# Splitting the weights anew in every block instead of keeping the split ones in HBM

## What is computed

```python
proj = rmsnorm(x, norm1_g) @ w_in                 # x_a | x_b | g_a | g_b, 1024 columns each
c_a = causal_conv4(x_a);  y_a = rg_lru(c_a)       # gates from 8 heads of 128x128, a scan in time
y_b = grouped_matmul(window_means(x_b) - x_b, pool_w) * scale   # windows 2, 4, 8, 16
x = x + (sigmoid(g_a) * (y_a @ w_br_a) + sigmoid(g_b) * (y_b @ w_br_b)) @ w_out
gu = rmsnorm(x, norm2_g) @ w_gu                   # 2 x 2816 columns
x = x + (silu(gu[:, :2816]) * gu[:, 2816:]) @ w_down
y = rmsnorm(x, final_g)
```

## Time and profile before

| | |
|---|---|
| median of 3 runs | 3032.33 us (3031.15 to 3035.28) |
| the profiled execution | 3035.47 us, span of its instructions 3033.7 us |
| PE busy | 2927.4 us, 96% of the span |
| PE weight loads | 2855.7 us, 94% |
| DVE busy | 1377.6 us, 45% |
| ACT busy | 797.9 us, 26% |
| POOL busy | 306.1 us, 10%, all in the first quarter |
| moved by DMA | 746.61 MB, mean 246 GB/s |

### The profile page before, as it was taken

One profiled execution on the slowest core, in us unless ns is written; L12 is line 12 of the kernel. 1 busy time (PEld: TensorE's weight loads), 2 busy tenths in 40 slices (PEclk: granted clock), 3 DMA queues, 4 the chain that ended last, 5 costly groups with the idle time before them and its releaser, 6 DMA issues.

```text
span 3033.7 us, 36581 instructions
## 1 busy us (share of the span) xinstructions
PE 2927.4 (96%) x15150; PEld 2855.7 (94%) x15150; DVE 1377.6 (45%) x2312; ACT 797.9 (26%) x1281; POOL 306.1 (10%) x134
## 2 busy tenths in 40 slices
PE   6789999899999999999999999999999999999998
PEld 6788998888999999999999999999999999999998
DVE  7426555556433334463434435533344363333334
ACT  4634323323511111152221102611111034111001
POOL 4344444440000000000000000000000000000000
PEclk9899999999999999999999999999999999999999
DMA  7688898897666666666666666766666676566664
GB/s 279 210 286 315 306 322 298 285 309 282 231 230 249 234 223 233 226 250 229 234 246 232 225 232 226 253 228 238 242 231 227 229 252 235 215 231 234 230 230 176
DMA packets 124579, 746.61 MB, mean 246 GB/s; under 512 B 14080, under 2 KB 24576, under 8 KB 46336
## 3 DMA queue, kind: packets, MB, share of 16 engines
q1 hardware_dynamic: 114048, 728.82, 66.7%
q10 hardware_dynamic: 10368, 15.46, 1.4%
HBM read 603.37 MB, written 140.86 MB: 245 GB/s over the span
## 4 chain that ended last, share of the span: by engine, by line
PE 78%; DMA 10%; POOL 4%; DVE 3%; ACT 3%; issue 1%; SPq 1%; DVEq 0%; ACTq 0%
PE ps L292 77%; DMA wraw<-dwm 10%; POOL wring L252 4%; ACT wring L401 2%; SPq L222 0%; DVE tmp L731 0%; PE ps L310 0%; DVE tot L632 0%; DVE tmp L646 0%; DVE xlo L650 0%; DVE tmp L700 0%; DMA wring<-wsplit 0%; DVE rstd L637 0%; ACT L455 0%; ACT L473 0%
## 5 line engine op out<-in xcount | busy, mean ns | idle before, releaser
L292 PE MATMUL ps<-yhi,wring 128*128 128x420 f32 (+1 forms) x4800 | 1324.9, 354 | 19.1 <-DVE main L763 6.9
L292 PEld LDWEIGHTS ps<-yhi,wring 128*128 128x128 f32 x4800 | 904.0, 188 | 41.7 <-issue 13.4
L292 PE MATMUL ps<-xhi,wring 128*128 128x420 f32 (+1 forms) x3200 | 891.9, 356 | 35.0 <-POOL wring L252 20.7
L292 PE MATMUL ps<-ylo,wring 128*128 128x420 f32 (+1 forms) x2400 | 848.3, 353 | 0.0
L292 PEld LDWEIGHTS ps<-xhi,wring 128*128 128x128 f32 x3200 | 606.6, 190 | 54.2 <-POOL wring L252 24.4
L292 PE MATMUL ps<-xlo,wring 128*128 128x420 f32 (+1 forms) x1600 | 568.2, 355 | 0.0
L292 PE MATMUL ps<-hhi,wring 128*128 128x420 f32 (+1 forms) x1760 | 491.5, 355 | 15.7 <-POOL wring L252 14.3
L292 PEld LDWEIGHTS ps<-ylo,wring 128*128 128x128 f32 x2400 | 451.9, 188 | 8.6 <-issue 1.3
L292 PEld LDWEIGHTS ps<-hhi,wring 128*128 128x128 f32 x1760 | 332.4, 189 | 25.2 <-POOL wring L252 18.9
L252 POOL TENSOR_TENSOR wring<-wraw,wring 128x1024 fp32r<-128x1024 f32 x122 | 294.9, 2420 | 382.6 <-ACT wring L401 382.6
L763 DVE TENSOR_TENSOR main<-ps,main 128x420 f32<-128x420 f32 (+1 forms) x440 | 250.8, 590 | 136.7 <-PE ps L292 135.8
(11 more groups left out here) (94 smaller groups left out, 1681.7 us busy)
## 6 DMA issues: line engine op xcount, KB each, us to landing
wring<-wsplit SPq DMA_DIRECT2D x488, 1024.0 KB, 4.8
wsplit<-wring SPq DMA_DIRECT2D x122, 1024.0 KB, 5.0
wraw<-dwm SPq DMA_DIRECT2D x122, 512.0 KB, 5.9
sring<-ssplit SPq DMA_DIRECT2D x32, 512.0 KB, 3.9
dy<-main ACTq DMA_DIRECT2D x32, 210.0 KB, 6.1
xres<-dx ACTq DMA_DIRECT2D x28, 210.0 KB, 4.7
ssplit<-sring SPq DMA_DIRECT2D x8, 512.0 KB, 6.8
sraw<-dws SPq DMA_DIRECT2D x8, 256.0 KB, 7.1
```

Of the source, the lines that this page charges most:

```text
L292: mm = nc.tensor.matmul(out, wt[:, c * P:(c + 1) * P], x, start=(first and q == 0), stop=(last and q == 2))
```

## The change

The HBM scratch is gone, with its stores and loads. Every block loads raw slots, now into three buffers, and splits them itself: the high part on ACT, the low part on POOL. The sides likewise. `ahead` works in every block. In the heads stage and the feed-forward part some of its calls move: the split for the slot four after `ga(2p)` comes before ACT's wait for the scans, the one for `gb(p-1)` before the square roots, the one for the first `g` before `root`. The normalization for the next block is done in two halves, in rounds 5 and 6 of the feed-forward part instead of all in round 5. The SP queue issues raw loads in order, each after POOL is done with the slot three before.

```diff
+RAW = 3
...
-        wraw = sb("wraw", [P, 2, KT * P])
+        wraw = sb("wraw", [P, RAW, KT * P])
...
             def raw(n):
-                if n >= 2:
-                    sp.wait_ge(w_lo, n - 1)
-                sp.dma_start(wraw[:, n % 2, :], dwm[n]).then_inc(raw_in[n % 2], 16)
...
-            def load(n):
-                sp.wait_ge(ready, slot_end(n - RING))
...
-                sp.dma_start(wring[:, n % RING].rearrange("p k c -> p (k c)").bitcast(f32), wsplit[n % NS]).then_inc(w_in[n % RING], 16)
...
+                if n >= RAW:
+                    sp.wait_ge(w_lo, n - RAW + 1)
+                sp.dma_start(wraw[:, n % RAW, :], dwm[n % NS]).then_inc(raw_in[n % RAW], 16)
...
-            for n in range(NS):
-                sp.wait_ge(w_lo, n + 1)
-                sp.dma_start(wsplit[n], wring[:, n % RING].rearrange("p k c -> p (k c)").bitcast(f32)).then_inc(w_saved[n % RING], 16)
...
+            for n in range(RAW, NB * NS):
+                for v in sides.get(n, ()):
+                    if v < NB * 8:
+                        side_raw(v)
+                raw(n)
...
-            for n in range(NS):
-                split_lo(n)
...
+            for n in range(3, NB * NS):
+                split_lo(n)
+                b, at = divmod(n, NS)
+                for p in range(4):
+                    if at == SLOT[("ga", 2 * p)] + 3:
+                        split_side(b * 8 + p + 2)
+                    if at == SLOT[("gb", 4 + p)] + 3 and b * 8 + p + 6 < NB * 8:
+                        split_side(b * 8 + p + 6)
...
             def ahead(b, s, i):
-                if b == 0 and SLOT[(s, i)] + RING < NS:
-                    split_hi(SLOT[(s, i)] + RING)
+                n = b * NS + SLOT[(s, i)] + RING
+                if n < NB * NS:
+                    split_hi(n)
...
-                if b == 0 and p + 2 < 8:
-                    split_side(p + 2)
+                split_side(b * 8 + p + 2)
...
+                if p:
+                    ahead(b, "gb", p - 1)
                 for j in range(2):
                     act.wait_ge(q_done, b * KT + 2 * p + j + 1)
                     A(tmp[:, 4 * j + 3, 0:bw], tmp[:, 4 * j + 3, 0:bw], ACT.Sqrt).then_inc(mult_done, 1)
+                ahead(b, "ga", 2 * p)
...
                 A(tmp[:, f % 2, 0:bw], tmp[:, f % 2, 0:bw], ACT.Silu).then_inc(silu, 1)
-                ahead(b, "g", f)
+                if f:
+                    ahead(b, "g", f)
...
                         sigmoid(("ga", b, 2 * p - 2), ga)
-                        ahead(b, "ga", 2 * p - 2)
                         sigmoid(("ga", b, 2 * p - 1), ga)
                         ahead(b, "ga", 2 * p - 1)
                         sigmoid(("gb", b, p - 1), gb)
-                        ahead(b, "gb", p - 1)
...
-                if b == 0:
-                    for m in range(KT):
-                        ahead(b, "a", m)
+                for m in range(KT):
+                    ahead(b, "a", m)
...
+                ahead(b, "g", 0)
                 root(("n2", b, 0), 1)
...
-                    if i and b == 0:
+                    if i:
                         ahead(b, "d", 2 * i - 2)
                         ahead(b, "d", 2 * i - 1)
...
-                    if i == 5 and not last:
-                        for k in range(KT):
-                            normed(b + 1, k)
+                    if i in (5, 6) and not last:
+                        for k in range(4):
+                            normed(b + 1, 4 * (i - 5) + k)
```

More of the change, by code:

```diff
@@ L90, in side_end, with side_before, build @@
     return JOB[("gi", b, 2 * q + 1) if q < 4 else ("pj", b, 2 * (q - 4) + 1)] + 1
-def side_slot(q):
-    return SLOT[("xa", 7)] if q == 0 else SLOT[("gb", q - 1 if q < 4 else q)]
+def side_before():
+    at = {6: [2, 3]}
+    for b in range(NB):
+        for p in range(4):
+            at.setdefault(b * NS + SLOT[("ga", 2 * p)] + 6 + RAW, []).append(b * 8 + p + 4)
+        for g in range(4):
+            at.setdefault(b * NS + SLOT[("gb", 4 + g)] + 4 + RAW, []).append(b * 8 + g + 8)
+    return at
 def upto(b, i, per, sampled):
     return (b * KT + i) * per + max(0, min((b - SB) * KT + i, KT)) * (sampled - per)
-def build(nc, dx, dwm, dws, dcst, dfix, dst0, dy, dst, wsplit, ssplit):
+def build(nc, dx, dwm, dws, dcst, dfix, dst0, dy, dst):
     f32 = mybir.dt.float32
@@ L139, in build @@
         x_in = [sem(f"x_in{k}") for k in range(KT)]
-        raw_in, sraw_in = [sem("raw_in0"), sem("raw_in1")], [sem("sraw_in0"), sem("sraw_in1")]
+        raw_in, sraw_in = [sem(f"raw_in{q}") for q in range(RAW)], [sem("sraw_in0"), sem("sraw_in1")]
         w_hi, w_lo, s_hi, s_lo = sem("w_hi"), sem("w_lo"), sem("s_hi"), sem("s_lo")
[L142 to L145, removed]
         y_stored, state_stored = sem("y_stored"), sem("state_stored")
@@ L219, in _ @@
                 sp.dma_start(dst_[:], src_).then_inc(tables_in, 16)
-            for n in range(NS):
-                sp.wait_ge(w_lo, n + 1)
-                sp.dma_start(wsplit[n], wring[:, n % RING].rearrange("p k c -> p (k c)").bitcast(f32)).then_inc(w_saved[n % RING], 16)
[L223 to L237, removed]
+            raw(2)
+            sides = side_before()
+            for n in range(RAW, NB * NS):
[3 more added lines that the diff above has]
+                raw(n)
             sp.wait_ge(h_saved, upto(NB, 0, 1, 2))
@@ L580, in _ @@
                     projected(b, g)
-                    if b == 0 and g + 2 < 4:
-                        split_side(g + 6)
+                    if b * 8 + g + 6 < NB * 8:
+                        split_side(b * 8 + g + 6)
                 for m in range(KT):
@@ L638, in invert, with normalize @@
                 dve.wait_ge(rstd_done[q], b + 1)
-            def normalize(b):
+            def normalize(b, first, count):
                 bw = BW[b]
-                for k in range(KT + 1):
-                    if k < KT:
+                for k in range(first, first + count + 1):
+                    if k < first + count:
                         if k >= 2:
@@ L770, in _ @@
             invert(("n1", 0, 0), 0)
-            normalize(0)
+            normalize(0, 0, KT)
             chain = [0]
@@ L863, in _ @@
                         invert(("n1", b + 1, 0), 0)
-                    if i == 5 and not last:
-                        normalize(b + 1)
+                    if i in (5, 6) and not last:
+                        normalize(b + 1, 4 * (i - 5), 4)
             invert(("n3", NB - 1, 0), 2)
```

71 lines of the change are left out of this document (23 added, 48 removed).

## The result

| | before | after |
|---|---|---|
| median, us | 3031.86 (4 runs, 3031.15 to 3035.28) | 3077.38 (4 runs, 3076.38 to 3077.92) |
| ratio | | 1.0146 [1.0131, 1.0161] |
| span of the profiled execution, us | 3033.7 | 3076.1 |
| DVE, ACT, POOL busy | 45%, 26%, 10% | 50%, 42%, 51% |
| moved by DMA | 746.61 MB | 350.32 MB |

The change makes the kernel 1.46% slower. 3090 was forecast.

What follows compares the result with a forecast made beforehand. PE bounds blocks 1 to 3; block 0 also waits for POOL and loads. Terms of 32.0 us per block, 128 for four, 134 with block 2's extra 6, less 75.5 in block 0, gave span 3092.2, time 3090 us, range 3000 to 3155.

Steps and rivals of the forecast that it cites:

- 1, `n3`: After the last `dn` product, an added split on ACT makes DVE's sums late; PE's column sum waits 1.5 us.
- Step 2: `xa` products: POOL holds DVE's steps, so ACT's sigmoid table load comes 19.2 us after the gates start, 13.4 late.
- T: The end of the last `dn` product, from which the forecast counts times in each of blocks 1 to 4.
- Step 3: First heads cycle: a side split adds 0.5 us and a POOL instruction before the second scan 2.4; 16.3 us late.
- Step 4: Three more heads cycles: ACT's cycle is 19.85 us against 14.27, 16.8 us in all; ACT bounds the stage.
- Step 5: Slack before `a`: the last scan's parts are ready at 1966.7 and needed at 1972.0, which takes off 5.3 us.
- Step 6: Before the end of `a0`: PE idles some 6 us, then runs at half clock for a while, +2.7 us.
- The moved splits: Heads cycles: one split moves into a 1.35 us wait; POOL holds the first scan pair 0.7 us, the second 2.1.
- What was held to be free: Feed-forward rounds, `b`, `o`, `gb` and `xb`: splits stay hidden; one may be 10 us late before PE sees it.
- Hidden after all: Rival, heads stage: DVE's lateness is absorbed, a block loses about 4 us, the kernel takes 2958; chance 0.15.
- Late splits stall PE in other stages: Rival: PE also stands outside the heads stage, 15 to 25 us more per block, 3150 to 3190; chance 0.12.
- three buffers are not enough: Rival: every block runs at block 0's pace, 5 x 678, 3400 us; chance 0.02.

Runs made afterwards that it cites:

- write_only_heads: The kernel after, but POOL writes zeros instead of subtracting for slots 12 to 23 and four sides, split in the heads stage: 3008.44 us, 0.992.
- old_places: The kernel after, with the heads stage's splits back at their old places in all five blocks: 3057.83 us, ratio 1.0084.
- write_only_21: The kernel after, but POOL writes zeros instead of subtracting for slots 3 to 23 and the heads stage's four sides: 2951.52 us, 0.9726.
- pool_write_long: The kernel after, but POOL writes zeros in three chained instructions per slot, busy about as long as with the subtraction: 2946.27 us, ratio 0.9717.

## Why the prediction was right

The sign, the place and the mechanism were right. By its own steps, for block 3:

| step | forecast | measured |
|---|---|---|
| 1, `n3` | +1.5 | +1.7 (PE's gap 1.87, before 0.19); `xa` window +1.8 |
| 2, table load late | 13.4 | 10.4 |
| 3, after the first cycle | 16.3 | 12.8 (cycle 16.74, before 14.33) |
| 4, three cycles | 19.85 each, +16.8 | 20.1 each, +17.6 |
| 5, slack before `a` | -5.3 | -5.7 |
| 6, clock | +2.7 | +1.6 |
| block 3 | +32.0 | +28.0 |
| block 2 beyond that | +6 | +5.6 |
| block 0 | 629.6 (its end) | 631.3 |

- *Step 2 was too large by 3.0 us.* I counted 6.4 us for each of the last three steps, as if POOL's 2.4 us were all added. They take 5.98: POOL starts while DVE is in its last L648 and a small copy, which it doesn't hold, and the first instruction behind is held. But the fifth step is 5.9 us long, where I had 4.8, and the first four differ both ways. The eight come to 44.2 us, forecast 44.3; that the sums agree is luck. With T at 1852.4 they start at T+10.7 (forecast 11.3) and end at T+54.9 (55.6). What I had wrong is what comes behind: I put 2.5 us between the eighth step and ACT's table load, a tail on DVE (to T+57.4) and 0.7. ACT waits for DVE's L648 alone, as the row above shows, and the load comes 0.5 us after the steps, at T+55.4 and not T+58.1. These 2.7 us, through step 3, are most of the difference in a block.
- *Step 3.* +2.4 and not +2.9.
- *Step 4 was right for a reason that lacked a part.* ACT's own work makes the cycle 16.69 (write_only_heads), where I had 17.05, and POOL adds 3.4, where I had 2.8. I had left out that the side's subtraction, 1.65 us, queues on POOL between two slots; it is what holds the scan (2.00 us instead of 1.09). That the scan can be held was in the forecast only by the rule of the Trainium skill (SBUF — State Buffer, Who interferes with whom); now a row shows it.
- *Step 5.* ACT's `ga` sigmoid behind the last scans comes 32.2 us later in the block than before (1984.94 against 1967.36, each from its block's start), PE's first matmul that needs their parts 26.4 us later; the slack takes up the difference.
- *Step 6.* The `a` window is 4.6 us longer: 3.0 are the wait, 1.6 are eleven matmuls that start 0.34 us apart in place of 0.19. The forecast had 8.3 us of waits in block 0's `a` window, where the earlier trace rows give 8.0 (48.90 - 40.88), so its term would be 2.85. In the heads stage 34 more matmuls run at half clock, for 5.4 us; each such stretch is followed by another wait of PE for ACT or DVE, so I count nothing for it; that is argued, not measured.
- *The moved splits* were counted at 1.85 us more per cycle than block 0's 18.0; old_places measures 2.0 (20.1 against 18.13), and as a whole 19.5 us.
- *What was held to be free was free*: the feed-forward windows, `xb`, `gb`, `b` and `o` keep their lengths, and write_only_21 puts all of the subtractions' price into the 21 slots of the `xa` and heads stages.
- *Hidden after all* fell: it needed a lateness on DVE that is absorbed. DVE's late steps do reach PE in full, beyond the slack.
- *Late splits stall PE in other stages* and *three buffers are not enough* had nothing in them but one wait of 1.9 us for POOL, in the `a` products of block 1; even two buffers do.
- *PE's waits* for ACT's `ga` sigmoids and for the parts before `a` were to be 25 to 30 us per block. They are 17.0 in block 3, and all waits 19.9: the forecast had counted ACT's lateness as waiting, and part of it is matmuls at half clock.
- *Raw loads*: under 5.7 us and no wait, as said; the 3.3 us were not foreseen.
- *A wrong detail*: L758 (L731 after) was to keep 597 ns beside POOL; it takes 829 in block 3. POOL's subtraction of one slot does reach the next L731 at times.

The sum: block 0 wins 73.9 us, where 19 us per block would have been break-even, and blocks 1 to 4 lose 25.6, 33.6, 28.0 and 29.1, together 116.3. The difference is 42.4, which is that of the spans, 3076.1 - 3033.7. (Block 1 before had 2.3 us of block 0's trouble left, hence 25.6.)

## What to carry to other kernels

A share of busy time does not say whether an engine can take more work: POOL at 50% was free in the feed-forward part and cost 26 us a block in two short stages where DVE had under a microsecond to spare in a step. Before work goes to POOL, look in each stage at the DVE instructions that would stand beside it, at what they read, and at how much slack their chain has. And take a change apart: here one more buffer in the kernel before gave all of the gain, and the rest of the change gave it back and more.

## What the runs showed of the hardware

- **Reading is what holds.** Beside POOL's subtraction DVE's two-input instructions wait for its end (L671 2.53 us for 0.59, the scan 2.00 for 1.09); beside writes of the same length they keep 592 and 1093 ns; with one operand in PSUM they keep 592 to 596 in both. The Trainium skill (SBUF — State Buffer, Who interferes with whom) has both halves: two SBUF inputs contend "with a GpSimd instruction that reads SBUF, not with one that only writes it". The trace agrees, for the scan too.
- **A copy of three columns is held as well**, 2.29 us by a subtraction, and also by writes. In pool_write_long, at a moment when POOL writes for 5.22 us:

```profile
1784.34 5.22 POOL L232 MEMSET wring<- 128x1024 f32 x6 [6.65 <-ACT wring L376]
...
1785.32 0.58 DVE L632 COPY tbuf<-state 128x3 f32<-128x3 f32 x1
...
1785.93 0.98 DVE L636 COPY state<-tbuf 128x3 f32<-128x3 f32 x1
1786.01 2.31 DVE L642 SCALAR_TENSOR_TENSOR gb<-tbuf,cst,gb 128x420 f32<-128x420 f32 x3
```

  The copies take 0.58 and 0.98 us, where both take 0.16 to 0.17 with POOL quiet, and each ends within 0.02 us of the end of one of POOL's writes. Of the three taps, which read two tensors, only the first, which starts under the held copy, is longer (0.91 us); the other two take 0.66 and 0.65 beside writes, as in quiet. The Trainium skill (SBUF — State Buffer, Who interferes with whom) says that a copy can enter a 2-port mode, when its operands meet certain conditions, and that it then contends with GpSimd. These rows agree with it. So the smallest instruction of a DVE chain can carry the longest wait.
- **It works both ways.** The subtraction of POOL that starts at 1938.07, while DVE's scan reads, takes 3.11 us instead of 2.4.
- **A 512 KB load lands in 3.3 us** where no 1 MB transfers run, in 5.9 beside the stores with two buffers, in 7.0 with three. More buffers made each load slower and block 0 still 77 us shorter.
